# Two trunk tiles first, W_o's evictions in another order, and tile 6's square added on VectorE

## What is computed

```python
def rmsnorm(x, g):
    xf = x.astype(jnp.float32)
    y = xf * lax.rsqrt(jnp.mean(xf * xf, axis=-1, keepdims=True) + RMS_EPS)
    return (y * g.astype(jnp.float32)).astype(x.dtype)

def swiglu(x, w_in, w_out):
    gate, up = jnp.split(x @ w_in, 2, axis=-1)
    return (jax.nn.silu(gate) * up) @ w_out
...
    for l in range(DEPTH):
        g = norm_g[l]
        h = h + 0.5 * rmsnorm(swiglu(rmsnorm(h, g[FFN1_PRE]), ffn_w_in[l, 0], ffn_w_out[l, 0]), g[FFN1_POST])
        hn = rmsnorm(h, g[MIX_PRE])
...
        h = h + rmsnorm(merged @ w_o[l], g[MIX_POST])
        h = h + 0.5 * rmsnorm(swiglu(rmsnorm(h, g[FFN2_PRE]), ffn_w_in[l, 1], ffn_w_out[l, 1]), g[FFN2_POST])
    return h[:, N_META:]
```

## Time and profile before

| what | value |
|---|---|
| runs, median (lowest to highest) | 1229.23 us (1226.35 to 1229.56) |
| the profiled execution's own time | 1229.71 us |
| its span | 1227.6 us |
| TensorE busy | 1200.9 us (98%), mean granted clock 0.994 |
| VectorE, ScalarE, GpSimd busy | 738.3, 538.9, 449.9 us |
| chain that ended last, shares by engine | TensorE 86%, VectorE 6%, ScalarE 4%, issue 2%, GpSimd 1% |

### The profile page before, as it was taken

One profiled execution on the slowest core, in us unless ns is written; L12 is line 12 of the kernel. 1 busy time (PEld: TensorE's weight loads), 2 busy tenths in 40 slices (PEclk: granted clock), 3 DMA queues, 4 the chain that ended last, 5 costly groups with the idle time before them and its releaser, 6 DMA issues.

```text
span 1227.6 us, 23903 instructions
## 1 busy us (share of the span) xinstructions
PE 1200.9 (98%) x9364; PEld 1165.2 (95%) x9364; DVE 738.3 (60%) x1020; ACT 538.9 (44%) x747; POOL 449.9 (37%) x527
## 2 busy tenths in 40 slices
PE   6999999999999999999999999999999999999997
PEld 5999999999899999999999999999988998999986
DVE  4755444768866575553467554447678766755543
ACT  5433334535654453334344333345366645443441
POOL 2645411204512266452117454112054123755600
PEclk9999999999999899999999999999999999999999
DMA  9655356473256455534646553564733663664540
GB/s 286 207 171 162 119 171 205 116 231 104 70 138 206 137 165 179 171 120 152 206 139 207 171 162 117 171 205 117 232 104 83 167 198 104 212 199 155 169 173 35
DMA packets 197597, 197.58 MB, mean 161 GB/s; under 512 B 4120, under 2 KB 190720, under 8 KB 197520
## 3 DMA queue, kind: packets, MB, share of 16 engines
q1 hardware_dynamic: 197232, 196.22, 50.7%
q10 hardware_dynamic: 288, 0.27, 0.1%
HBM read 195.42 MB, written 1.05 MB: 160 GB/s over the span
## 4 chain that ended last, share of the span: by engine, by line
PE 86%; DVE 6%; ACT 4%; issue 2%; POOL 1%; DMA 0%; SPq 0%; DVEq 0%; ACTq 0%; POOLq 0%
PE bank L437 26%; PE bank L439 25%; PE bank L438 25%; ACT w_hi L833 2%; PE bank L619 2%; PE bank L620 2%; PE bank L618 2%; DVE w_lo L1076 2%; PE bank L513 1%; PE bank L523 1%; DVE s L1300 1%; DVE x_lo L1140 1%; DVE stats L1304 1%; DVE h L1158 1%; PE bank L707 1%
## 5 line engine op out<-in xcount | busy, mean ns | idle before, releaser
L1076 DVE TENSOR_TENSOR w_lo<-raw,w_hi 128x2048 fp32r<-128x2048 f32 (+3 forms) x208 | 439.0, 2116 | 285.3 <-ACT w_hi L833 285.3
L437 PE MATMUL bank<-x_hi,w_hi 128*128 128x272 f32 (+1 forms) x2028 | 589.2, 291 | 6.4 <-DVE w_lo L1076 4.4
L439 PE MATMUL bank<-x_hi,w_lo 128*128 128x272 f32 (+1 forms) x2028 | 582.6, 287 | 0.0
L438 PE MATMUL bank<-x_lo,w_hi 128*128 128x272 f32 (+1 forms) x2028 | 580.8, 286 | 0.0
L833 ACT ACTIVATE w_hi<-raw 128x2048 fp32r<-128x2048 f32 (+2 forms) x212 | 355.6, 1686 | 446.9 <-PE bank L439 435.1
L437 PEld LDWEIGHTS bank<-x_hi,w_hi 128*128 128x128 f32 x2028 | 383.2, 189 | 10.6 <-DVE w_lo L1076 4.8
L438 PEld LDWEIGHTS bank<-x_lo,w_hi 128*128 128x128 f32 x2028 | 383.2, 189 | 0.3
L439 PEld LDWEIGHTS bank<-x_hi,w_lo 128*128 128x128 f32 x2028 | 383.1, 189 | 0.0
L437 PE MATMUL bank<-hid_hi,w_hi 128*128 128x272 f32 x528 | 152.9, 290 | 0.0
L438 PE MATMUL bank<-hid_lo,w_hi 128*128 128x272 f32 x528 | 152.2, 288 | 0.0
L439 PE MATMUL bank<-hid_hi,w_lo 128*128 128x272 f32 x528 | 151.5, 287 | 0.0
(11 more groups left out here) (185 smaller groups left out, 1252.5 us busy)
## 6 DMA issues: line engine op xcount, KB each, us to landing
raw<-in_ffn_w_in SPq DMA_DIRECT2D x88, 1024.0 KB, 5.1
raw<-in_w_in SPq DMA_DIRECT2D x24, 1024.0 KB, 5.5
raw<-in_ffn_w_out SPq DMA_DIRECT2D x24, 768.0 KB, 4.4
raw<-in_ffn_w_out SPq DMA_DIRECT2D x24, 640.0 KB, 4.0
raw<-in_ffn_w_out SPq DMA_DIRECT2D x10, 1024.0 KB, 5.1
raw<-in_w_in SPq DMA_DIRECT2D x16, 512.0 KB, 4.8
raw<-in_w_attn_proj SPq DMA_DIRECT2D x32, 256.0 KB, 4.4
raw<-in_w_o SPq DMA_DIRECT2D x8, 1024.0 KB, 5.3
```

Of the source, the lines that this page charges most:

```text
L437: pe.matmul(ps[:, t0:T], w[0], a_hi[:, t0:T], start=start, stop=False)
L438: pe.matmul(ps[:, t0:T], w[0], a_lo[:, t0:T], start=False, stop=False)
L439: return pe.matmul(ps[:, t0:T], w[1], a_hi[:, t0:T], start=False, stop=stop)
L1076: last = dve.tensor_tensor(lo, w, hi.bitcast(F32), ALU.subtract)
```

## The change

The post-norm's sums become two groups: VectorE adds tile 6's square to GpSimd's sum (`add_square_6`), in the middle of a weight split, and the first group is issued before the last product. At W_o VectorE copies tiles 4 to 6 before splits 67 and 68, and ScalarE squares tiles 4 and 5 before split 67. In the trunk VectorE does h of tiles 0 and 1 before the first x_lo, and from then on h, tmp of the next tile, x_lo of the same tile; ScalarE does x_hi of tile k+1 before the square of tile k. GpSimd's five adds of a post-norm stay.

```diff
--- before.py
+++ after.py
@@ -59,8 +59,8 @@
 END_K = (2, 4, 4, 4, 4, 4)
 END_K0 = (0, 2, 6, 10, 14, 18)
 N_END = 2 * len(END_K)
-SUM_PARTS = (1, 3)
-ADDS = (KD - 1, KD - 3)
+SUM_PARTS = (1, 2)
+ADDS = (KD - 1, KD - 2)
 TOKENS = (0, P, T - P)
 PAD = POOL_WINDOWS[-1]
 
@@ -507,8 +507,8 @@
                         pe.wait_ge(r_ready, l * 3 + q // 2 + 1)
                     pe.wait_ge(acc_done, adds_to(n + 1))
                 else:
-                    pe.wait_ge(sq_done, (n + 1) * KD + part - 2)
-                src = acc[:, :] if part == 0 else sq[:, part - 1, :]
+                    pe.wait_ge(sq_done, (n + 1) * KD)
+                src = acc[:, :] if part == 0 else sq[:, (KD - 1) % 2, :]
                 for b, first in enumerate(TOKENS):
                     last = pe.matmul(small[:, S_SUM + b:S_SUM + b + 1], src[:, first:first + P], ones[:, 0:1],
                                      start=(part == 0 and b == 0), stop=(part == SUM_PARTS[q % 2] - 1),
@@ -569,18 +569,16 @@
                     for mt in range(2):
                         if j == 0:
                             tile_free(tile0 + u // 4 * 2 + mt, l, 4)
-                        if u == N_OUT - 1 and mt == 1:
-                            sum_part(4 * f + 1, l, 0)
                         for k in range(OUT_K[j]):
                             kk = OUT_K0[j] + k
                             if u == N_OUT - 1 and mt == 1 and kk == KF - 1:
-                                sum_part(4 * f + 1, l, 1)
+                                sum_part(4 * f + 1, l, 0)
                             last = products(bank[2 * pair + mt], weights(u0 + u, k, mt), hid_hi[:, kk, :],
                                             hid_lo[:, kk, :], kk == 0, kk == KF - 1, t0)
                         if mt == 0 and j == 3:
                             last.then_inc(first_done, 1)
                     last.then_inc(unit_done, 1)
-                sum_part(4 * f + 1, l, 2)
+                sum_part(4 * f + 1, l, 1)
                 keep_warm(WARM_RMS)
                 spread_rms(4 * f + 1, l)
                 keep_warm(WARM_X)
@@ -780,13 +778,9 @@
                 tile_free(T_WO + 6, l, 4)
                 unit_tile(U_WO + 3, l, 0, 2, KD, x_hi, x_lo, t0)
 
-                def sums_so_far():
-                    sum_part(3, l, 0)
-                    sum_part(3, l, 1)
-
                 tile_free(T_WO + 7, l, 4)
-                unit_tile(U_WO + 3, l, 1, 3, KD, x_hi, x_lo, t0, before_last=sums_so_far)
-                sum_part(3, l, 2)
+                unit_tile(U_WO + 3, l, 1, 3, KD, x_hi, x_lo, t0, before_last=lambda: sum_part(3, l, 0))
+                sum_part(3, l, 1)
                 keep_warm(WARM_RMS)
                 spread_rms(3, l)
                 keep_warm(WARM_X)
@@ -858,8 +852,10 @@
 
             def pre_norm(n, columns, h_before):
 
+                x_high(columns, h_before, 0)
                 for k in range(KD):
-                    x_high(columns, h_before, k)
+                    if k + 1 < KD:
+                        x_high(columns, h_before, k + 1)
                     square(n, k, h[:, k, :], h_ready, h_before + k + 1)
 
             def silus(f, l, pair, more=0):
@@ -1046,11 +1042,11 @@
                 split_hi(66, l)
                 for m in range(4):
                     square(l * NORMS + 3, m, y[:, m, :], tile_read, l * TILES + T_WO + m + 1 + TR0)
-                split_hi(67, l)
                 for m in range(4, 6):
                     square(l * NORMS + 3, m, y[:, m, :], tile_read, l * TILES + T_WO + m + 1 + TR0)
+                split_hi(67, l)
+                square(l * NORMS + 3, 6, y[:, 6, :], tile_read, l * TILES + T_WO + 6 + 1 + TR0)
                 split_hi(68, l)
-                square(l * NORMS + 3, 6, y[:, 6, :], tile_read, l * TILES + T_WO + 6 + 1 + TR0)
                 last_square(l * NORMS + 3, bank[3], l * UNITS + U_WO + 4 + RING)
                 take_root(l * NORMS + 3)
                 pre_norm(l * NORMS + 4, g_cur[:, 4 * KD:5 * KD], l * 3 * KD + 2 * KD)
@@ -1134,6 +1130,13 @@
                 dve.tensor_copy(r[:, :], small[:, S_BC:S_BC + T]).then_inc(r_ready, 1)
                 dve.wait_ge(r_ready, l * 3 + q // 2 + 1)
 
+            def add_square_6(q, l):
+
+                n = l * NORMS + q
+                dve.wait_ge(acc_done, adds_to(n) + KD - 3)
+                dve.wait_ge(sq_done, n * KD + KD - 1)
+                dve.tensor_tensor(acc[:, :], acc[:, :], sq[:, 0, :], ALU.add).then_inc(acc_done, 1)
+
             def x_low(at, columns, k):
 
                 dve.wait_ge(xhi_ready, at + k + 1)
@@ -1157,13 +1160,12 @@
                     dve.wait_ge(t_ready, l * 3 * KD + n * KD + k + 1)
                     dve.scalar_tensor_tensor(out=h[:, k, :], in0=tmp[:, k % 2, 0:T], scalar=1.0 if n == 1 else 0.5,
                                              in1=h[:, k, :], op0=ALU.mult, op1=ALU.add).then_inc(h_ready, 1)
-                    if k >= 2:
-                        x_low(at, columns, k - 1)
+                    if k == 1:
+                        x_low(at, columns, 0)
                     if k + 1 < KD:
                         normed(k + 1)
-                    if k == 0:
-                        x_low(at, columns, 0)
-                x_low(at, columns, KD - 1)
+                    if k >= 1:
+                        x_low(at, columns, k)
 
             def take_gate(f, l, unit, mp=0):
 
@@ -1215,13 +1217,13 @@
                 if f == 0:
                     split_lo(U_K, l)
                     split_lo(U_V, l)
-                    take_out(3, between=lambda: split_lo(U_Q, l))
+                    take_out(3, between=lambda: split_lo_between(U_Q, l, lambda: add_square_6(1, l)))
                     post_rms(1, l)
                     boundary(0, l, l * 4 * KD + KD, g_cur[:, 2 * KD:3 * KD])
                 else:
                     split_lo(0, l + 1)
                     split_lo(1, l + 1)
-                    take_out(3, between=lambda: split_lo(2, l + 1))
+                    take_out(3, between=lambda: split_lo_between(2, l + 1, lambda: add_square_6(5, l)))
                     post_rms(5, l)
                     boundary(2, l, l * 4 * KD + 4 * KD, g_next)
 
@@ -1439,15 +1441,18 @@
                 merge_lo(7, l)
                 split_lo(65, l)
 
+                def split_two():
+                    split_lo_between(67, l, lambda: add_square_6(3, l))
+                    split_lo(68, l)
+
                 def take_y(n):
                     b = 2 * (n % 2)
                     take(U_WO + n, F_WO + n, l, (b, b + 1), lambda j, ps: dve.tensor_copy(y[:, 2 * n + j, :], ps),
-                         (l * NORMS + 4) * KD if n == 3 else None, (lambda: split_lo(68, l)) if n == 3 else None)
+                         (l * NORMS + 4) * KD if n == 3 else None, split_two if n == 3 else None)
 
                 take_y(0)
                 take_y(1)
                 split_lo(66, l)
-                split_lo(67, l)
                 take_y(2)
                 take_y(3)
                 post_rms(3, l)
@@ -1529,7 +1534,7 @@
                                pattern=[[-1, P]], channel_multiplier=1).then_inc(consts, 1)
 
             def add_squares(q, l):
-                for m in range(1, ADDS[q % 2] + 1):
+                for m in range(1, ADDS[q % 2] + 1 - q % 2):
                     pool.wait_ge(sq_done, (l * NORMS + q) * KD + m + 1)
                     if m == 1:
                         pool.wait_ge(ssq_done, l * NORMS + q + 1)
```

## The result

The changed kernel takes 1239.03 us (median of 4 runs, 1238.31 to 1239.91) against 1228.47 us: ratio 1.0086, 95% interval 1.0070 to 1.0102. It is slower, by 10.6 us or 0.9%, where 7.0 (1236.2 against 1229.2) was forecast; the profiled execution took 1238.34 us with a span of 1236.6 us, 9.0 over the original's.

The account below looks back on a forecast made before the run. The prediction took TensorE, nearly all of the chain of work, as the bound. Its terms at five boundaries summed to +6.7 us on the profiled execution's 1229.7, so 1236.4, stated as 1236.2 for the median; range 1222 to 1242.

Parts of the forecast that it names:

- The trunk (part 4): Trunk at each pre-norm: GpSimd's add holds each h, tile cycle 2.0 us, TensorE +1.3 us, last square +2.5 us.
- A, C, B, D, E: A, D: FFN to mixer (+1.9 us each); C, E: mixer to FFN (-0.1, +0.4); B: layer 0 to 1 (+2.6).
- The estimate of 0.5 for A and D's bank: FFN-to-mixer boundaries: weight splits stand ahead of r and kT, which release a bank; 0.5 us on top of 1.3.
- The add at the FFN ends (part 2): FFN ends: the group removed is paid back by TensorE's 0.8 us wait for VectorE's 0.44 us add; net +0.1 us each.
- W_o (part 3): W_o's ends: no wait, one group saved, clock stays up; gains of 2.6 us in layer 0, 2.1 in layer 1.
- the term of the clock: W_o's ends: TensorE's clock taken as staying up, 1.7 us more gain in layer 0; no fall counted at FFN ends.
- the third rival: The forecast holds, but the clock falls at the FFN ends, each up to 1.7 us: 1238 to 1241; chance 0.07.
- The forecast's last step: From the profiled execution's 1236.4 us to the median of the runs, 0.5 below that execution, stated as 1236.2.
- The first, h ahead of GpSimd: Trunk: h takes the ports before GpSimd, tile cycle 1.45 us, total 1222.4 us; chance 0.20.
- The second, uneven ties: Trunk: ties fall unevenly, one or two tiles held in each boundary, 0.55 us per held tile: 1225 to 1233; chance 0.14.
- The fourth, ports held to the end of a record: Trunk: ports held to each record's end, 1.5 us more at each of five boundaries, about 1243; chance 0.03.

Follow-up runs that it names:

- the trunk alone: The original kernel with only the change's two trunk orders (VectorE's and ScalarE's); 1240.62 us, ratio 1.0095.
- W_o alone: The original kernel with only the change's W_o part, three groups kept at the FFN ends; 1225.35 us, ratio 0.9966.
- three groups with the late add: The original with the change's W_o part and trunk orders, GpSimd's pre-norm add also waiting for the next tile's x_lo, three groups at FFN ends; 1222.55 us.
- the late add: The changed kernel plus one wait: GpSimd's pre-norm add of a square also waits for x_lo of the next tile; 1224.56 us, ratio 0.9958.
- the early add: The changed kernel with the late add, and at the FFN ends VectorE's add of tile 6's square ahead of the whole split; 1221.70 us, ratio 0.9938.
- Filled waits: The changed kernel plus three warming matmuls before the first group at FFN ends and three before the last group at all boundaries; 1235.65 us, ratio 1.0048.
- two experiments: The changed kernel plus GpSimd's pre-norm add waiting for the next tile's x_lo, 1224.56 us; the changed kernel plus a one-column memset before each such add, 1223.70 us.
- two profiles: Warming matmuls put in TensorE's waits: on the kernel with the late add and the early add, 1219.92 us; on the changed kernel, 1235.65 us.

## Why the prediction was right

**The trunk (part 4)** decided, as said, and by the mechanism said: GpSimd's add starts 0.05 us before h, five tiles in each boundary are held, 25 of 25. The cycle was 2.02 us for a forecast 2.0; the last square 14.76 after the first tmp for 14.75. Passed on were 1.76, 2.52, 2.49, 2.04 and 2.48 us (A, C, B, D, E), together 11.3, for 1.8, 2.5, 2.5, 1.8 and 2.5. In A TensorE's last wait for x_lo ended 14.70 us after the first tmp, with one tile of 1.5 to go, so 16.2 for 16.15; before, it ended at 10.37 with three to go, 14.9. The estimate of 0.5 for A and D's bank fits A (0.46 over 1.3) and is 0.24 short at D; the wait for kT that it stands on is there, 0.16 us at A and 0.52 at D, and in the original it isn't.

**The add at the FFN ends (part 2)**: 0.43 us for 0.44, TensorE's wait 0.80, net 0.17 for 0.1 where the clock stayed (B).

**W_o (part 3)**: 2.61 at C for 2.6. At E 2.23 where the clock stayed up, for 2.1, but 1.70 in the changed kernel, where it fell.

**What failed** is the term of the clock. The sum has nothing for a fall: at W_o's ends it took the clock as staying up, "as in all three of those", the FFN ends of the original, and at the FFN ends themselves it left a fall to the third rival. It fell at A (0.40 us) and D (1.37), and at E cost 0.53. That is the third rival (0.07) in two of three places, and the measured 1239.03 lies where its range (1238 to 1241) and the forecast's own (1233 to 1240) overlap: the forecast's mechanism with part of that rival's on top. Its condition, the wait for the add, was too narrow as well. In the four profiles of kernels with the original's three groups (the original, the trunk alone, W_o alone, three groups with the late add) the clock fell at 4 of 12 FFN ends; in the seven with two groups and nothing in the waits, at 10 of 21. The counts are read from the table, against +0.17 where it stayed up (-0.31 with the early add), and are too few to say that the wait makes a fall more likely. Filled waits show the forecast's own sum: 0.17 + 0.17 + 0.17 - 2.60 - 2.23 + 1.70 + 2.51 + 2.50 + 2.06 + 2.49 = 6.9 us, for 6.7. The changed kernel's own row of the table adds up to 9.3, the falls being the difference of 2.3 and a little more; a start 0.3 shorter brings it to the span's 9.0, and the two profiled executions' own times differ by 8.6. The rest up to 10.6 lies between executions: the changed kernel's median is 0.7 above its profiled execution, and the original's 1228.47 is 1.2 below the 1229.71 of its profiled execution, which is of another set of runs. The changed kernel's four runs lie at 1238.3 (two) and at 1239.7 and 1239.9, all with a granted clock of 0.995, so nothing shows that the clock tells them apart. The forecast's last step has a slip besides: 1236.4 less 0.5 is 1235.9, not 1236.2.

**The rivals.** The first, h ahead of GpSimd, didn't come by itself, but two experiments brought it about: 1224.6 and 1223.7 with falls, against 1222.4 for it; its gains after the first tmp were, with the late add, 1.1 at A and 0.7 at D for 0.9 worked out, 0.4 at B for 0.2, 0.2 at C and 0.4 at E for 0.3. The second, uneven ties, didn't come. The fourth, ports held to the end of a record, is excluded by the cycle of 2.02. The Trainium skill's SBUF — State Buffer (the two separate sides) is right that the one that starts first shuts out the other; its "whole instruction" is too long by the runs, since GpSimd's late add, asked at 229.46 in the run above, took 0.85, not 0.77, so was let in some 0.3 us after h began, while h's record is 0.43 long.

## What to carry to other kernels

When two engines compete for a port, as VectorE and GpSimd do here, and the next request of each hangs on the same third engine, compare the times of the two requests, not the loads. A lead of 0.05 us decided 14 to 15 us here, and it repeats in every turn, because the loser's delay is passed to both. Make the engine that is off the critical path ask later: by a wait on something that ends just after the critical instruction has begun, or even by a dummy instruction. And where two steps are merged and the engine then waits for the merged operand, the step isn't saved: place the producer of that operand first. If the clock falls around such waits, fill them.

## What the runs showed of the hardware

- GpSimd's add, out of a wait, and VectorE's h, directly behind another instruction, with records that begin 0.05 or 0.06 us apart: the earlier one, the add, won 25 times of 25. Directly behind a memset, an add with a lead of 0.01 or 0.02 us lost 20 times of 20. VectorE's two-tensor op of 0.44 us let GpSimd in after 0.30; GpSimd's add of 0.77 us held VectorE's for 0.58.
- A pattern of three engines can lock in phase: five tiles running at 2.02 us each, where the late add let the same work go at TensorE's pace.
- TensorE's granted clock fell to 1.2 GHz at ends of sub-layers in some kernels and not in others with the same instructions there, costing 0.4 to 1.7 us each; with identity matmuls in the waits of 0.3 to 0.8 us it fell at none of ten. These are two profiles, and the timed runs agree (1.8 and 3.4 us less than without, granted clock 0.998 to 1.000 in all ten). What makes the same instructions fall in one kernel and not in another stays open.
